# A mixture-of-experts kernel on one core: experts with at most 32 rows take four 32-column groups of the array

## The reference, cut to what matters

```python
logits = xt @ router_w + router_b                # 256 x 32
top_v, top_e = lax.top_k(logits, 4)              # 4 experts a token
gate = softmax(top_v)
# for each expert e, over the rows (tokens) that chose it:
hb = xb @ w1[e] + b1[e]                          # 1024 -> 2048
g, u = hb[:, :1024], hb[:, 1024:]
g = minimum(g, 7); u = clip(u, -7, 7)
glu = g * sigmoid(g * 1.702)
y = ((u + 1) * glu) @ w2[e] + b2[e]              # 1024 -> 1024
out[token] += y * gate
```

## Time and profile before

| | us |
|---|---|
| median of three runs | 2230.92 |
| the profiled execution | 2230.52 |
| its span, first to last instruction | 2228.7 |
| PE busy in it | 2094.6 (94%) |
| VectorE, ScalarE busy | 701.0 (31%), 448.4 (20%) |
| 16 DMA engines, weights queue | 70.0% of the span |
| HBM read | 587.48 MB, 265 GB/s over the span |
| expert stage | from about 442 to about 1434 |

### The profile page before, as it was taken

How to read it: one execution, slowest core, us unless ns; L and a number is a source line. 1 busy time by engine, 2 the same in 40 slices (tenths; PEclk the granted TensorE clock), 3 DMA queues, 4 the chain that set the end, 5 groups by cost and what they waited for, 6 DMA issues and landing times.

```text
span 2228.7 us, 28718 instructions
## 1 busy us (share of the span) xinstructions
PE 2094.6 (94%) x10964; PEld 1204.8 (54%) x10965; DVE 701.0 (31%) x1479; ACT 448.4 (20%) x874; POOL 0.2 (0%) x4
## 2 busy tenths in 40 slices
PE   6999989899989999999999999899999999999997
PEld 3767757433333333333333333376489976648996
DVE  2333223311110111111111111214267753525776
ACT  1322230100000000000000000112245431114543
POOL 0000000000000000000000000000000000000000
PEclk9999989899989999999999999999999999999999
DMA  9254674499978999999999979963166645432652
GB/s 357 89 172 167 227 195 149 186 376 426 424 282 338 425 425 426 425 426 425 426 425 426 424 274 426 366 164 104 29 187 181 184 127 144 139 104 86 196 171 84
DMA packets 189021, 590.95 MB, mean 265 GB/s; under 512 B 10571, under 2 KB 110466, under 8 KB 152996
## 3 DMA queue, kind: packets, MB, share of 16 engines
q1 hardware_dynamic: 186940, 587.68, 70.0%
q10 hardware_dynamic: 2024, 2.46, 0.4%
HBM read 587.48 MB, written 2.62 MB: 265 GB/s over the span
## 4 chain that ended last, share of the span: by engine, by line
PE 76%; DMA 17%; DVE 3%; ACT 2%; issue 1%; SPq 0%; ACTq 0%; DVEq 0%
DMA lower<-in_exp_w 16%; PE psum L1756 15%; PE psum L1941 11%; PE psum L1407 7%; PE psum L1780 6%; PE psum L1953 5%; PE psum L1509 5%; PE psum L1514 5%; PE psum L1541 3%; PE psum L1488 2%; PE psum L1800 2%; PE psum L1724 2%; PE psum L1494 1%; PE psum L1415 1%; PE psum L1749 1%
## 5 line engine op out<-in xcount | busy, mean ns | idle before, releaser
L1756 PE MATMUL psum<-lower,upper 128*64 128x512 f32 x2176 | 487.6, 602 | 25.6 <-DMA lower<-in_exp_w 25.6
L1756 PEld LDWEIGHTS psum<-lower,upper 128*64 128x64 f32 x2176 | 150.9, 137 | 362.4 <-issue 308.2
L1941 PEld LDWEIGHTS psum<-rounded 128*128 128x128 f32 x2112 | 258.6, 189 | 3.4
L1941 PE MATMUL psum<-rounded 128*128 128x256 f32 x2112 | 260.1, 283 | 0.0
L1780 PE MATMUL psum<-upper 128*64 128x512 f32 x1088 | 240.5, 595 | 6.8 <-ACT upper L1176 6.8
L2402 DVE TENSOR_SCALAR upper<-psum 128x512 f32<-128x512 f32 x34 | 23.5, 691 | 692.8 <-PE psum L1756 690.9
L1407 PE MATMUL psum<-upper,lower 128*128 128x256 f32 (+1 forms) x880 | 166.4, 389 | 4.1 <-ACT upper L971 4.1
L1780 PEld LDWEIGHTS psum<-upper 128*64 128x64 f32 x1088 | 75.3, 137 | 149.8 <-issue 137.0
L1407 PEld LDWEIGHTS psum<-upper,lower 128*128 128x128 f32 (+1 forms) x880 | 130.5, 174 | 35.6 <-issue 10.5
L1953 PE MATMUL psum<-rounded 128*128 128x512 f32 x528 | 128.9, 392 | 2.4 <-DVE rounded L2598 2.4
L1171 ACT ACTIVATE upper<-upper 128x512 f32<-128x512 f32 x32 | 20.1, 629 | 496.1 <-DVE upper L2402 496.1
(11 more groups left out here) (374 smaller groups left out, 1794.1 us busy)
## 6 DMA issues: line engine op xcount, KB each, us to landing
lower<-in_exp_w SPq DMA_DIRECT2D x128, 2048.0 KB, 21.4
upper<-in_exp_w SPq DMA_DIRECT2D x128, 1024.0 KB, 20.2
lower<-in_ffn_w_up SPq DMA_DIRECT2D x88, 512.0 KB, 5.3
lower<-in_mod_w SPq DMA_DIRECT2D x12, 2048.0 KB, 10.5
lower<-in_w_in SPq DMA_DIRECT2D x12, 2048.0 KB, 9.7
lower<-in_ffn_w_down SPq DMA_DIRECT2D x44, 512.0 KB, 5.7
lower<-in_odd_w_in SPq DMA_DIRECT2D x8, 2048.0 KB, 11.7
lower<-in_even_w_in SPq DMA_DIRECT2D x7, 2048.0 KB, 11.8
```

Source lines behind the costliest of these rows:

```text
L1756: ins = pe.matmul(bank[first_bank + r // 2][64 * half:64 * half + 64], rows, w1[k][:, 512 * r:512 * r + 512], start=False, stop=(k == W1_O ...
L1941: ins = pe.matmul(bank[4 + b][:, T * g:T * g + T], w[:, g, k, :], x[:, k, :], start=(k == m == 0), stop=(k == KD - 1 and m == 2))
```

## The change

Four edits go together.

- A third path, `few_rows_pass`, for experts with at most `FEW` = 32 rows. Its first layer sends quarter r of the hidden columns to the 32-column group r of the array, all four into bank 4, with a stationary operand of 128 x 32. Its bias comes after the first chunk.
- Its second layer also has four groups: two halves of the output columns by two chunks of a pair. Even and odd chunks are summed apart, into rows 0 to 31 and 32 to 63 of each half of bank 6. To add the two parts, every slot below 32 appears twice for such an expert: a second table `slot_two` is `slot_of` less 32 where the expert has more than 32 rows, and `slot_of` itself where it has not. `make_select` compares slots 0 to 31 with both tables.
- Quarter r now is 256 gate and 256 up columns (`gate_and_up`), for all experts. So with at most 32 rows, the whole activation lies in one bank; with more, gate and up columns share both banks. `activation` reads them by a view over the two banks, and the bias is loaded in the same order.
- The order of quarters in the paths for more rows is 0, 2, 1, 3, with the half r // 2 and the bank first + r % 2.

```diff
+FEW = 32
...
-                        sp.dma_start(exp_b1[0:P:32, :], a["exp_b1"][0, which, :].rearrange("o (r n) -> (o r) n", r=4))\
+                        sp.dma_start(exp_b1[0:P:32, :].rearrange("p (g n) -> p g n", g=2),
+                                     a["exp_b1"][0, which, :].rearrange("o (g r n) -> (o r) g n", g=2, r=4))\
...
+            def gate_and_up(k, r):
+                return w1[k].rearrange("p (g r n) -> p g r n", g=2, r=4)[:, :, r, :]
+
             def hidden_chunk(rows, k, first_bank=4):
 
-                for r in range(4):
-                    half = r % 2
-                    ins = pe.matmul(bank[first_bank + r // 2][64 * half:64 * half + 64], rows,
-                                    w1[k][:, 512 * r:512 * r + 512], start=False, stop=(k == W1_ORDER[-1]),
+                for r in (0, 2, 1, 3):
+                    half = r // 2
+                    ins = pe.matmul(bank[first_bank + r % 2][64 * half:64 * half + 64].rearrange("p (g n) -> p g n", g=2),
+                                    rows, gate_and_up(k, r), start=False, stop=(k == W1_ORDER[-1]),
                                     tile_position=(0, 64 * half))
                 return ins
+
+            def few_hidden_sums(e):
+
+                pe.wait_ge(b1_in, 16 * e + 16)
+                for k in W1_ORDER:
+                    pe.wait_ge(w1_in[k - k % 2], 16 * e + 16)
+                    rows, first, last = gathered_rows(k)[:, 0:FEW], k == W1_ORDER[0], k == W1_ORDER[-1]
+                    for r in range(4):
+                        ins = pe.matmul(bank[4][32 * r:32 * r + 32].rearrange("p (g n) -> p g n", g=2), rows,
+                                        gate_and_up(k, r), start=first, stop=last, tile_position=(0, 32 * r))
+                    if first:
+                        for r in range(4):
+                            ins = pe.matmul(bank[4][32 * r:32 * r + 32], ones[32 * r:32 * r + 1, 0:FEW],
+                                            exp_b1[32 * r:32 * r + 1, :], start=False, stop=False,
+                                            tile_position=(32 * r, 32 * r))
+                    ins.then_inc(w1_used, 1)
...
+            def few_output_sums(e):
+
+                pe.wait_ge(hiddenT_ready, e + 1)
+                for r in range(4):
+                    pe.wait_ge(w2_in[2 * r], 16 * e + 16)
+                    for half in range(2):
+                        for part in range(2):
+                            at = 64 * half + 32 * part
+                            ins = pe.matmul(bank[6][at:at + 32], hiddenT[:, part, 32 * r:32 * r + 32],
+                                            w2[2 * r + part][:, 512 * half:512 * half + 512], start=(r == 0), stop=(r == 3),
+                                            tile_position=(0, at))
+                            if half:
+                                ins.then_inc(w2_used, 1)
...
+            def few_rows_pass(e):
+
+                few_hidden_sums(e)
+                next_rows(e)
+                turn_hidden(bank[6], hidden_ready, e + 1, hidden_turned, 2)
+                turn_gathered(e + 2)
+                few_output_sums(e)
...
                 with pe.Else():
-                    one_pass(e)
+                    with pe.If(count > FEW):
+                        one_pass(e)
+                    with pe.Else():
+                        few_rows_pass(e)
...
+            chained(dve.tensor_scalar(over_few, counts[:, 0:N_EXP], float(FEW), float(FEW), ALU.is_gt, ALU.mult))
+            dve.tensor_tensor(slot_two[:, :, 0:N_EXP], slot_of[:, :, 0:N_EXP],
+                              over_few.rearrange("p (o e) -> p o e", o=1).to_broadcast([P, NT, N_EXP]), ALU.subtract)
...
                 for i in range(NT):
-                    where = slot_of[:, i, 0:1] if isinstance(n, int) else slot_of[:, i, bass.ds(n, 1)]
-                    ins = dve.tensor_scalar(select[:, i, :], iota[:, 0:SLOTS], where, None, ALU.is_equal)
+                    for part, place_of in enumerate((slot_of, slot_two)):
+                        where = place_of[:, i, 0:1] if isinstance(n, int) else place_of[:, i, bass.ds(n, 1)]
+                        ins = dve.tensor_scalar(select[:, i, FEW * part:FEW * part + FEW], iota[:, 0:FEW], where, None,
+                                                ALU.is_equal)
...
+                sums_of = psum[:, 512 * first_bank:512 * first_bank + 1024].rearrange("p (b g n) -> p b g n", b=2, g=2)
                 dve.wait_ge(hidden_sem, sums)
-                dve.tensor_scalar(gate_part, bank[first_bank], 7.0, None, ALU.min).then_inc(gate_sem, 1)
-                dve.tensor_scalar(up_part, bank[first_bank + 1], 7.0, -7.0, ALU.min, ALU.max).then_inc(own_steps["clipped"], 1)
+                dve.tensor_scalar(gate_part.rearrange("p (b n) -> p b n", b=2), sums_of[:, :, 0, :], 7.0, None,
+                                  ALU.min).then_inc(gate_sem, 1)
+                dve.tensor_scalar(up_part.rearrange("p (b n) -> p b n", b=2), sums_of[:, :, 1, :], 7.0, -7.0, ALU.min,
+                                  ALU.max).then_inc(own_steps["clipped"], 1)
```

More of the change, by code:

```diff
@@ L325, in program @@
         chosen, gates_t = arena.take(64, 32), arena.take(64, 32)
-        slot_of = arena.take(2 * (N_EXP + 1), N_EXP + 1)
+        slot_of, slot_two = arena.take(2 * (N_EXP + 1), N_EXP + 1), arena.take(2 * (N_EXP + 1), N_EXP + 1)
+        over_few = arena.take(N_EXP)
         id_gate = arena.take(NT * (N_EXP + 1) * 2, N_EXP + 1, 2)
@@ L1746, in hidden_bias @@
                 pe.wait_ge(b1_in, 16 * e + 16)
-                for r in range(4):
-                    half = r % 2
-                    pe.matmul(bank[first_bank + r // 2][64 * half:64 * half + 64], ones[32 * r:32 * r + 1, 0:SLOTS],
+                for r in (0, 2, 1, 3):
+                    half = r // 2
+                    pe.matmul(bank[first_bank + r % 2][64 * half:64 * half + 64], ones[32 * r:32 * r + 1, 0:SLOTS],
                               exp_b1[32 * r:32 * r + 1, :], start=True, stop=False, tile_position=(32 * r, 64 * half))
+            def gate_and_up(k, r):
+                return w1[k].rearrange("p (g r n) -> p g r n", g=2, r=4)[:, :, r, :]
@@ L1769, in hidden_sums, with turn_hidden @@
                 return ins
-            def turn_hidden(o, ready, n, done):
+            def turn_hidden(o, ready, n, done, chunks=4):
                 pe.wait_ge(ready, n)
-                for j in range(4):
+                for j in range(chunks):
                     ins = pe.transpose(o[:, P * j:P * j + P], of_chunk(hidden, j), ident)
@@ L2331, in _ @@
             dve.memset(slot_of[:, :, N_EXP:N_EXP + 1], -1.0)
+            dve.memset(slot_two[:, :, N_EXP:N_EXP + 1], -1.0)
             dve.memset(y_sb, 0.0).then_inc(y_ready, 1)
```

## The result

The changed kernel takes 2259.72 us (median of 4 runs, 2258.93 to 2264.61), beside 2229.63 us (4 runs, 2223.82 to 2231.58) for the kernel before on the same chip: ratio 1.0152, 95% interval 1.0134 to 1.017. It is 30 us slower, where 10 us faster was forecast, and outside the range given.

The account below looks back on a forecast made before the run. DMA was taken as the bound, 29.68 us an expert against TensorE's 27.33, except at start and end. Gains of 1.9 + 1.8 + 6.4 = 10.1 us from 2230.52 gave 2220.4, as a median 2220.8 us; range 2215 to 2235.

Parts of the forecast that it names:

- Code loading: Rival: three paths no longer stay loaded, so e27 and e28 pay 7 us each; 2235 us, chance 0.06.
- (1): Start of the expert stage: e0 releases its first weight buffers 1.9 us sooner, between 1 and 2.5.
- (2): Up to e6: TensorE's 1.8 us lag behind landed weights at e5 closes; e6 begins 3.7 us sooner overall.
- F: TensorE's cost of an expert with at most 32 rows: 17.8 us after the change, from 27.33.
- No four at once: Rival: the four column groups do not run together, records stay at 0.218 us; 2236 us, chance 0.11.
- (3): e7 to e26: DMA runs without a gap at 29.69 us each, so 0 more is gained.
- The clock rival: Waits for weights drop TensorE to half clock, costing 5 us at each of e5, e26 and e31; 2236 us, chance 0.12.
- (4): End of the expert stage: two experts of few rows close TensorE's 6.4 us lag behind e31's weights, gaining 6.4 us.
- The other edits at 0: Halved rows for larger experts, two-bank reads, eight-piece bias load and larger selections across the expert stage: costed at 0.

Follow-up runs that it names:

- e27: Not a run: expert 27 of the stage's 32, 79 rows, two passes; 61.33 us in the kernel before, 71.85 in the changed kernel.
- few_never: The changed kernel with the third path's code present but never taken; 2268.27 us, ratio 1.0187 to the kernel before.
- one_copy: The changed kernel with the never-entered further pass held once, in a loop, instead of twice; 2217.14 us, ratio 0.995 to the kernel before.
- e28: Not a run: expert 28, 45 rows, one pass; 29.25 us in the kernel before, 41.34 in the changed kernel.
- e7: Not a run: expert 7, above 32 rows, one pass; 29.47 us in the kernel before, 40.00 in the changed kernel.
- before_long: The kernel before with a third copy of the never-entered further pass, 1842 instructions in TensorE's loop instead of 1528; 2225.88 us, ratio 0.9998.
- end_pad_47: The kernel before with 192 instructions that never run placed behind the one-pass path; 2264.63 us, ratio 1.017.
- end_pad_59: The kernel before with 240 instructions that never run placed behind the one-pass path; 2263.39 us, ratio 1.0165.
- common_first: one_copy with the branches turned round, paths for at most 64 rows first and the two-pass path last; 2211.21 us, ratio 0.9933 to the kernel before.
- e0: Not a run: expert 0, the first of the stage's 32, at most 32 rows.
- before_first: The kernel before with the path for up to 64 rows placed first in TensorE's loop; 2245.84 us, ratio 1.0095.
- first_never: common_first with the path for at most 32 rows present but never taken; 2225.94 us, ratio 0.9993 to the kernel before.
- e5: Not a run: expert 5, above 32 rows, one pass; ends at 608.71 us in the kernel before, 615.71 in the changed kernel.
- e29: Not a run: expert 29, at most 32 rows.
- e4: Not a run: expert 4, above 32 rows, one pass.
- e26: Not a run: expert 26, above 32 rows, one pass.
- e8: Not a run: expert 8, at most 32 rows; the 19 experts from it to e26 take 550.89 us before, 550.91 in the changed kernel.
- layout_only: The changed kernel without its third path, keeping two-bank layout, doubled slots and four-column selections; 2229.32 us, ratio 1.0014 to the kernel before.
- e6: Not a run: expert 6, 79 rows, two passes; 72.09 us in both the kernel before and the changed kernel.
- e31: Not a run: expert 31, the last of the stage's 32, above 32 rows, one pass.
- end_pad_28: The kernel before with 116 instructions that never run placed behind the one-pass path; 2224.21 us, ratio 0.999.
- e1: Not a run: expert 1, at most 32 rows.

## Why the prediction was wrong, step by step

**The step that failed** is the rival "Code loading", which had a chance of 0.06. "Against: e27 showed no such stand after 20 other experts" takes a row of a loop of 1528 instructions as evidence about one of 1806; that row says only that the shorter loop is kept. The added path was priced by its durations, and its instructions were never counted or laid out. Its condition ("if three paths no longer stay loaded") was the right one; few_never shows it by itself, and one_copy takes it away.

**Its size was wrong too**: 14 us in two experts for 33.1 in three. I counted the return at e28 but not that at e7, since before e7 shows no stand; a stand at the return is 8.2 to 8.3 us, not 7; and an expert loses 10.5 to 12.1 us for stands of 7.7 to 8.3. The 2 to 4 us between are the clock. In and behind each new stand it is at 1.2 GHz (10.2 us after 692.66 in e7, 13.65 us after 1354.85 in e28, 20.5 us after 1283.17 in e27, where before had 10.2), while PE is the path. Profiles of the same path in other kernels give the price. e27 without a stand takes 58.28 us in before_long (3.4 us of it at 1.2 GHz) and 61.33 in before (10.2). e28 takes 39.67 us in end_pad_47 (a stand of 7.98, then 4.9 us at 1.2 GHz) and 41.31 in end_pad_59 (8.19, then 7.9). That is 0.45 to 0.5 us for each us at 1.2 GHz. Behind the stand lie 5.0 of these us in e7 and 7.9 in e28, an estimated 2.2 to 2.5 and 3.6 to 4.0 us, for the 2.2 and 3.9 found. With 33 us for 14 the rival would have said 2254, next to the 2259.72 measured; the rest is the start, (1) and (2).

**(1) The start**, forecast 1.9 us sooner. In after the first new weight load is issued 7.6 us later, not sooner:

```profile
457.87 6.60 SPq L824 DMA_DIRECT2D lower<-in_exp_w  x4
```

Of the 7.6, 3.2 is how late this execution reached the routing ahead of the stage (L1347 at 409.68 us, L1344 at 406.46 before), 2.2 that L1848 ran in part at 1.2 GHz (5.87 us for the 3.70 of its counterpart in the earlier trace rows), 3.3 the longer code stand (7.94 for 4.63); first matmul to issue gives 1.2 back (6.75 for 7.93). In common_first, where no stand is in the way, first matmul to issue is 6.16 us for 7.93: 1.8 sooner, as worked out. Beside the two kernels with the old path and no stand in e0 it is 1.2 (before_first, 7.40) and 2.9 (first_never, 9.09); these two differ in where the clock is at 1.2 GHz, so the term is right to about 1 us.

**(2) The lag up to e5**, forecast 1.8 us. From the first issue to e5's end is 158.43 us before, 157.84 in after, 158.18 in one_copy, 157.95 in common_first: only 0.2 to 0.6. F itself was right: its records take 0.111 us (6.22/56) in the first layer and 0.114 (3.64/32) in the second, in e29:

```profile
1391.90 0.60 ACT L1200 ACTIVATE upper<-psum 128x512 f32<-128x512 f32 x1 [7.19 <-PE psum L1802]
...
1393.77 6.22 PE L1774 MATMUL psum<-lower,upper 128*32 128x512 f32 x56
...
1405.24 3.64 PE L1824 MATMUL psum<-upper 128*32 128x512 f32 x32 [0.21 <-ACT upper L1179]
1408.98 0.60 ACT L1200 ACTIVATE upper<-psum 128x512 f32<-128x512 f32 x1 [3.79 <-PE psum L1824]
```

An unblocked one takes 1408.98 - 1391.90 = 17.08 us (forecast 17.8). "No four at once" is refuted. What was off is the count of the landing (590.8 for e5's last first-layer pair): e4 and e5 do wait for their pairs, and these come about 1.3 us later than I counted. Whether that is the 2.0 us of latency or the rate in this stretch is not separated.

**(3) e7 to e26 at 0.** Right from e8 on, by the windows of these 19 experts, before and after:

```profile
710.27:1261.16 550.89, 521.27 (x2585) 178.03 (x2586) 85.28 (x189) 45.99 (x76) 0.00 (x0) 1.00 1.01 426
```
```profile
727.80:1278.71 550.91, 439.15 (x2560) 128.53 (x2557) 90.10 (x225) 46.12 (x76) 0.00 (x0) 0.93 1.01 426
```

The clock rival is refuted there. PE is at 1.2 GHz for some 78 us of them (none before), and they cost nothing more, since DMA holds the path. e7 is the reload's.

**(4) The end**, forecast 6.4 us of lag closed: 6.1 in after, 6.05 between first_never and common_first. Right.

**The other edits at 0**: layout_only has 0.14% [0.01%, 0.27%], some 3 us, which no expert's pace shows (27.34 to 27.35 us for 27.33).

**What the change is worth without the reload**: with one copy of the extra pass 0.995 [0.993, 0.9969], with the common paths first 0.9933 [0.991, 0.9956]. That the first is about the 10 us forecast is in part luck. In its profiled execution the stage ends 9.1 us sooner than in before: e5 ends 7.5 later (the stand of 10.0 us in e0), e6 takes 10.8 less, and only the 6.0 from e28's end to e31's are a term of the sum. Likewise common_first ends 18.0 us sooner, of which 7.5 are e6, 3.0 the clock in e27 and 6.0 the end. So of the terms for a loop that is kept, the end (6.4 forecast, 6.0 to 6.1 found) and the steady part (0) are shown, the start (1.9) to about 1 us, and the lag at e5 (1.8) was mostly not there.

## What to carry to other kernels

A path added to a loop with branches costs its code as well as its time: count the engine's instructions in blocks of 256 over all that the loop touches, and look in the DMA rows for instruction packets inside the loop. A row that shows code kept holds for the program it was read from, not for a longer one. Before rejecting a good change for a stand that shows as "issue", shrink or move code that never runs: here one loop in place of two copies turned +30 us into -9, and the order of the branches decided whether a stand that stays falls where work hides it.

## What the runs showed of the hardware beyond that

- 76 instructions that never execute cost about 40 us (end_pad_28 against end_pad_47), and 314 that never execute cost nothing where they are jumped over ahead of the rest (before_long).
- TensorE at 1.2 GHz for 78 of the 551 us of e8 to e26 added nothing, where the weights' DMA sets the pace at 29 us an expert. Where TensorE is the path, each us at 1.2 GHz cost 0.45 to 0.5 us (e27 in before_long and before, e28 in end_pad_47 and end_pad_59).
- A first-entry stand is moved rather than removed when its block is reached another way: from e0 to e1 in common_first (5.5 us) and before_first (3.6 us).
